# A hybrid decoder step on one core: quarter tiles for the sample attention, and its steps between k chunks of the second gate

## The chip, the cores and the metric

The kernel runs on one core of a Trainium2 chip. The metric is device time in microseconds (us), from the start to the end of one execution. TensorE (PE) multiplies, VectorE (DVE) and ScalarE (ACT) work elementwise, GpSimd (POOL) works elementwise and starts indirect DMAs, SyncE (SP) starts the weight loads. PE reads operands from SBUF and writes to eight PSUM banks: PS[0] and PS[1] of two banks each and PB of four.

## The reference, cut to what matters

One inference step of a decoder with two layers, of 512 + 16 prompt rows and 8 x 4 sample rows. Every sample row attends to the 256 best of 2048 cached keys and the new ones, which an index score picks; the cache is paged and is read through a page table. For the gates:

```python
z = x @ w_in
q, k, v, qi, ki, wi, h, bg, cg, ga, gb = jnp.split(z, offs, axis=-1)
u = cg * h                                   # convolved along the rows, times bg
logits = jnp.einsum('bqngd,bqjnd->bqngj', qg, kg).astype(jnp.float32) * (HEAD_DIM ** -0.5)
p = jax.nn.softmax(logits, axis=-1).astype(vg.dtype)
o = jnp.einsum('bqngj,bqjnd->bqngd', p, vg)
```

The attention's result times w_attn_out is multiplied with sigmoid(ga), the convolution's times w_conv_out with sigmoid(gb); the sum goes through w_o, a layer norm and a squared-ReLU MLP.

## The kernel before, in words

x (560 columns: 528 prompt rows and 32 sample rows) is kept transposed, split in a high and a low part (AXh, AXl). Every weight product is a *unit* (unit, L489 to L508): 128 output columns, 48 matmuls of 128x280, from 3 products of high and low parts, 8 k chunks and 2 halves of the rows. A weight slice of 512 KB is loaded by SP (load, L319), cast to its high part WH by ACT (high, L946) and subtracted to its rest WL by POOL (rest, L393), through two slots s = 0, 1. A unit of slot s writes PS[s], and the next one in that slot waits until it is evacuated (evac_done).

A layer runs through P1, keys and values, the queries of all heads, index scores, the prompt's top-k, GA (first gate), then the **head loop** (8 heads), the **conv stage** (w_conv_out, 8 units), the **sample attention**, AO (w_attn_out), WO and the MLP. Every engine has its own queue, in which the order is written out by hand; semaphores join them.

The head loop (PE L693 to L762, ACT L1153 to L1218, DVE L1580 to L1676): each head does the prompt attention of five row tiles (p_logits L713 and L714, p_transposes L726, p_values L738 on PE; p_exp, p_norm, p_out on ACT; p_max, p_inv, p_turned on DVE), with four units between: h, cg, bg and gb (the second gate) , all four of the same group of 128 columns. DVE multiplies h by cg (gate_c, L1627), convolves (short_conv, L1639 to L1643), multiplies by bg and splits (gate_b, L1648, L1404, L1405) into AHh and AHl. ACT turns gb into 1 + exp(-gb) in BB. DVE also does three of the 32 steps of the sample rows' top-k in each head (a pair of s_top L1572 and s_take L1575 on 32 x 2080 scores), four pairs before the loop and four in the conv stage. In the conv stage DVE does the reciprocals of BB (L1690) and multiplies the products by it (L1701).

The sample attention (PE L776 to L863) goes over g = 0, 1, four sequences each. POOL gathers (L439) the keys and then the values into KVB, two half tiles of 4 x 1 MB, which lie in AXh and AXl (h = 0) and in AHh and AHl (h = 1). PE transposes the keys into three banks (L797), ACT and DVE take turns at copying them to KTR (L1243, L1723), PE makes logits (L810, eight steps q), adds masks (L818) and the new keys (L826, L829); after DVE's maximum and ACT's exp come transposes of P (L838), values (L854) and transposes of the result (L861). DVE splits the result for AO (L1715, L1757, L1758); SG holds the first gate, whose reciprocals DVE does in this stage (L1690, L1725).

Of the kernel before, what the change touches and what calls it, by code (L numbers as in the profile page):

```python
# [22 lines left out]
P = 128  # L23
# [46 lines left out]
QH, GA, GATES, CONV, AO, WO, MLP = -1, 0, 1, 5, 6, 7, 8  # L70
# [14 lines left out]
def gate_use(k, c):  # L85


    return k % 2, c * 2 + (phase_use(k % 2, GATES) + k // 2)


def gate_slot_use(k, c):

    return c * 2 + (slot_use(GATES) + k // 2)
# [47 lines left out]
def trunk_program(nc, a):  # L141
    with ExitStack() as ctx:
# [10 lines left out]
        def at(name, shape, dt, off):  # L153
# [8 lines left out]
        KVB = [[at(f"KVB{h}{b4}", [P, TPP // 2, KV_W], F32, (off_axh, off_axl, off_ahh, off_ahl)[2 * h + b4 // 2]  # L162
                   + b4 % 2 * (TPP // 2 * KV_W * 4)) for b4 in range(4)] for h in range(2)]
# [82 lines left out]
        IDXH = sb("IDXH", [P, 2, NB], U32)  # L246
# [6 lines left out]
        HALF = [PS[i // 2][:, i % 2, 0:RH] for i in range(4)]  # L253
        V1 = PB[:, 2:4, 0:RH]
# [33 lines left out]
        kv_in = [[sem(f"kv_in{h}{b4}") for b4 in range(4)] for h in range(2)]  # L288
        kt_t, kt_ea, kt_ed, kt_mm = sem("kt_t"), sem("kt_ea"), sem("kt_ed"), sem("kt_mm")
# [18 lines left out]
        rows_k = a["cache_k"].rearrange("l n (s t) h d -> (l n s) (t h d)", t=TPP // 2)  # L308
        rows_v = a["cache_v"].rearrange("l n (s t) h d -> (l n s) (t h d)", t=TPP // 2)
# [8 lines left out]
        def _(sp):  # L318
# [32 lines left out]
            for l in range(DEPTH):  # L351
# [16 lines left out]
                with sp.Fori(0, KC) as c:  # L368
                    for k, col in enumerate((COL_H, COL_CG, COL_BG, COL_GB)):
                        s, n = gate_use(k, c)  # L370
                        load(s, l * USES[s] + n, wcol(w_in_v, l, c * P + col))
                for name, ph in (("w_conv_out", CONV), ("w_attn_out", AO), ("w_o", WO)):
# [19 lines left out]
        def _(pool):  # L392
# [12 lines left out]
            for l in range(DEPTH):  # L405
# [23 lines left out]
                with pool.Fori(0, 4 * (CONV + 1)) as i:  # L429
                    for s in range(2):  # L430
                        rest(s, l * USES[s] + i + phase_use(s, QH), s)
                for s in range(2):
                    rest(s, l * USES[s] + phase_use(s, CONV), s)

                def gather(g, h, rows):

                    for b4 in range(4):
                        b = 4 * g + b4
                        pool.indirect_dma_start(KVB[h][b4][:].rearrange("p t d -> p (t d)"), None, rows,  # L439
                                                bass.IndirectOffsetOnAxis(ap=IDXH[:, h, b:b + 1], axis=0)  # L440
                                                ).then_inc(kv_in[h][b4], 16)

                def products_done(ph):
                    for s in range(2):
                        pool.wait_ge(mm_done[s], l * SLOT_USES[s] + slot_use(ph) + 1)
                        apart(pool, started)

                products_done(CONV)
                gather(0, 0, rows_k)
                with pool.Fori(0, 3) as i:  # L450
                    for s in range(2):
                        rest(s, l * USES[s] + i + (phase_use(s, CONV) + 1), s)
                for s in range(2):
                    rest(s, l * USES[s] + phase_use(s, AO), s)
                products_done(AO)
                gather(0, 1, rows_k)
                for g in range(2):
                    if g == 1:
# [1469 lines left out]
```

## Time and profile before

| | us |
|---|---|
| time, three runs | 2591.24, 2593.61, 2595.88 (median 2593.61) |
| the profiled execution | 2593.55 |
| its span in the trace | 2591.8 |
| PE busy | 2324.9 (90%) |
| DVE busy | 1497.8 (58%) |
| ACT busy | 795.7 (31%) |
| POOL busy | 792.2 (31%) |

The profiled execution's own time is its span and 1.75 us around it. The page gives busy times of the engines, what the chain of work that ended last consists of, the costliest groups of instructions and the landing times of DMAs; the stages are told apart by windows of the trace, the order inside one by the timeline and the chain of waits. "PEclk" is the clock granted to TensorE, as a share of the full 2.4 GHz.

### The profile page before, as it was taken

The page shows a single profiled execution, that of the slowest core. Times are in us where ns is not written, and L with a number is a line of the kernel's source. Part 1 is how long each engine was busy: PE and PEld are TensorE (multiplying, and loading weights), DVE is VectorE, ACT ScalarE, POOL GpSimd, SP SyncE. Part 2 cuts the span into 40 slices and gives each one's busy share as a digit, 9 for nine tenths or more (in the row PEclk, how much of TensorE's full clock was granted, in tenths as well). Part 3 has the DMA queues.
Part 4 walks back from the last instruction along what each step waited for, and adds up shares of the span by engine and source line. Part 5 has one row for each costly group of instructions (what it writes and reads, how often), then busy time and mean ns, then how long its engine had stood idle before and what let it go on. Part 6 is the DMA issues. An engine that isn't in the chain of part 4 may idle for free.

```text
span 2591.8 us, 45648 instructions
## 1 busy us (share of the span) xinstructions
PE 2324.9 (90%) x17159; PEld 2134.2 (82%) x17159; DVE 1497.8 (58%) x2234; ACT 795.7 (31%) x1379; POOL 792.2 (31%) x384
## 2 busy tenths in 40 slices
PE   5988999998669899999899889999975899999995
PEld 4965988888339899999898489888953699999995
DVE  3759877778556632132586797777856566132145
ACT  2233333331111332222242443333221125122233
POOL 2410322234214323333443022222331252343440
PEclk9977999999779999999999699999997899999998
DMA  4420222225632322323333022222464232223230
GB/s 117 132 61 16 67 64 57 57 60 200 260 130 77 87 57 82 89 82 89 109 116 95 6 59 56 64 57 57 138 226 189 94 100 68 73 82 89 82 97 35
DMA packets 321366, 238.03 MB, mean 92 GB/s; under 512 B 9560, under 2 KB 309576, under 8 KB 313080
## 3 DMA queue, kind: packets, MB, share of 16 engines
q1 hardware_dynamic: 304424, 154.69, 21.5%
q0 software_dynamic: 12032, 77.07, 7.5%
q10 hardware_dynamic: 4816, 4.96, 0.6%
q8 instruction: 67, 1.10, 0.2%
q14 instruction: 27, 0.22, 0.0%
HBM read 231.73 MB, written 4.96 MB: 91 GB/s over the span
## 4 chain that ended last, share of the span: by engine, by line
PE 78%; DVE 11%; ACT 4%; issue 3%; DMA 2%; ACTq 1%; SPq 0%; DVEq 0%; POOL 0%; POOLq 0%
PE PS L504 54%; PE PS L489 9%; PE PS L797 3%; DVE BB L1690 2%; PE PB L714 2%; PE PS L623 2%; PE PB L738 2%; PE PB L810 1%; PE PS L854 1%; DVE SG L1690 1%; DVE SG L1725 1%; DVE SQ L1430 1%; DMA KVB<-in_cache_v_dram,IDXH 1%; DVE TKS L1575 1%; PE PB L726 1%
## 5 line engine op out<-in xcount | busy, mean ns | idle before, releaser
L395 POOL TENSOR_TENSOR WL<-ST,WH 128x1024 fp32r<-128x1024 f32 x290 | 705.2, 2433 | 1539.0 <-ACT WH L949 1539.0
L949 ACT CAST WH<-ST 128x1024 fp32r<-128x1024 f32 x290 | 303.7, 1047 | 1099.5 <-PE PS L504 944.1
L504 PE MATMUL PS<-AXh,WH 128*128 128x280 f32 x2688 | 575.6, 296 | 21.0 <-DVE AXl L1758 12.6
L504 PE MATMUL PS<-AXl,WH 128*128 128x280 f32 x2688 | 571.5, 294 | 0.0
L504 PE MATMUL PS<-AXh,WL 128*128 128x280 f32 x2688 | 566.5, 292 | 0.0
L504 PEld LDWEIGHTS PS<-AXh,WH 128*128 128x128 f32 x2688 | 432.0, 190 | 23.0 <-issue 21.6
L504 PEld LDWEIGHTS PS<-AXl,WH 128*128 128x128 f32 x2688 | 432.8, 191 | 0.0
L504 PEld LDWEIGHTS PS<-AXh,WL 128*128 128x128 f32 x2688 | 428.1, 190 | 0.0
L504 PE MATMUL PS<-AHh,WH 128*128 128x280 f32 x1152 | 242.0, 291 | 3.6 <-DVE AHl L1823 3.4
L504 PE MATMUL PS<-AHl,WH 128*128 128x280 f32 x1152 | 243.2, 292 | 0.0
L504 PE MATMUL PS<-AHh,WL 128*128 128x280 f32 x1152 | 241.0, 290 | 0.0
L1822 DVE TENSOR_TENSOR MT<-MT 128x560 f32<-128x560 f32 (+1 forms) x76 | 96.4, 1268 | 238.1 <-ACT AHh L1317 217.0
L504 PEld LDWEIGHTS PS<-AHh,WH 128*128 128x128 f32 x1152 | 182.9, 188 | 4.7 <-DVE AHl L1823 3.8
L504 PEld LDWEIGHTS PS<-AHl,WH 128*128 128x128 f32 x1152 | 183.7, 189 | 0.0
L504 PEld LDWEIGHTS PS<-AHh,WL 128*128 128x128 f32 x1152 | 181.7, 188 | 0.0
L797 PEld LDWEIGHTS PS<-ident,KVB 128*128 128x128 f32 x512 | 69.5, 166 | 103.3 <-DVE KTR L1723 42.8
L1782 DVE TENSOR_TENSOR X<-X,PS 128x560 f32 (+2 forms) x60 | 37.2, 620 | 201.8 <-PE PS L504 165.2
L797 PE MATMUL PS<-ident,KVB 128*128 128x128 f32 x512 | 84.8, 323 | 75.5 <-DVE KTR L1723 39.8
L1572 DVE MAX8 top<-TKS 32x8 f32<-32x2080 f32 x64 | 147.3, 2302 | 3.2 <-DVE TKS L1575 2.9
L1575 DVE MATCH_REPLACE8 TKS<-top,TKS 32x2080 f32<-32x2080 f32 x64 | 147.0, 2297 | 0.0
L489 PE MATMUL PS<-AXh,WH 128*128 128x280 f32 x384 | 119.1, 310 | 19.3 <-DVE AXl L1447 10.0
L489 PE MATMUL PS<-AHh,WH 128*128 128x280 f32 x384 | 116.3, 303 | 3.8 <-issue 3.8
(249 smaller groups left out, 3476.9 us busy)
## 6 DMA issues: line engine op xcount, KB each, us to landing
ST<-in_w_in_dram SPq DMA_DIRECT2D x114, 512.0 KB, 3.8
ST<-in_w_up_dram SPq DMA_DIRECT2D x64, 512.0 KB, 4.0
ST<-in_w_down_dram SPq DMA_DIRECT2D x64, 512.0 KB, 3.8
ST<-in_w_conv_out_dram SPq DMA_DIRECT2D x16, 512.0 KB, 3.8
ST<-in_w_attn_out_dram SPq DMA_DIRECT2D x16, 512.0 KB, 3.7
ST<-in_w_o_dram SPq DMA_DIRECT2D x16, 512.0 KB, 3.8
NAT<-in_x_prompt_dram SPq DMA_DIRECT2D x4, 512.0 KB, 3.7
o_y_dram<-NAT ACTq DMA_DIRECT2D x4, 512.0 KB, 2.6
```

The lines of the kernel that those rows point to most:

```text
L395: pool.tensor_tensor(WL[slot][:, :, :], ST[s][:, :, :], WH[slot][:, :, :].bitcast(F32), ALU.subtract).then_inc(lo_done[s], 1)
L489: mm = pe.matmul(out, x[:, k, :], y[:, k, r0:r1], start=(k == 0 and y is hi and x is WH[slot]), stop=(k == KC - 1 and y is lo))
L504: mm = pe.matmul(out[:, h, 0:RH], x[:, k, :], y[:, k, RH * h:RH * h + RH], start=(k == 0 and y is hi and x is WH[slot]), stop=(k == KC - 1 ...
L623: mm = pe.matmul(PS[j % 2][0:n, k0 // 512, 0:k1 - k0], x[hp, c0:c0 + n], y[hp, k0:k1], start=(i == 0), stop=(i == 2))
L714: mm = pe.matmul(bank, QST[:, c0:c0 + m], KT[:, n, k0:k1], start=False, stop=True)
L738: mm = pe.matmul(PB[:, 3, 0:m], VN[0:k1, kt, HD * n:HD * n + HD], PPT[i % 2][0:k1, m * kt:m * kt + m], start=(kt == 0), stop=(kt == keys(r ...
L797: tr = pe.transpose(banks[t % 3][:, P * j:P * j + P], KVB[c // 2][b4][:, 4 * (c % 2) + j, HD * n:HD * n + HD], ident[:, :])
L949: act.copy(WH[slot][:, :, :], ST[s][:, :, :]).then_inc(hi_done[s], 1)
L1572: own.link(dve.max(top[0:RS, 0, :], TKS[:, :]), alone=True)
L1575: own.link(dve.match_replace(TKS[:, :], top[0:RS, 0, :], TKS[:, :], NEG_TAKEN), alone=True)
L1690: own.link(dve.reciprocal(v, v))
L1822: own.link(dve.tensor_tensor(h, h, h, ALU.mult))
```

## The change

The second gate's products (gb) leave the head loop, whose heads come in pairs now, with three units each cut at k chunks (6 matmuls of 128x280 each) and in another order on all engines. DVE's top-k pairs are moved: none before the loop, two in even heads and three in odd ones, twelve in the conv stage. ACT copies conv's products to BB. The 64 k chunks of the gb units are laid between the steps of the sample attention, all through PS[0]; ACT's exp goes to a buffer GE, DVE does its reciprocal and multiplies BB by it. Keys and values are gathered in quarter tiles (16 of 4 x 0.5 MB a layer instead of 8 halves of 4 x 1 MB) through two buffers in AHh and AHl, since AXh and AXl are wanted by the gb products; POOL's gathers wait for the last reader of a buffer, and the rests of the gb weights stand between them. All copies to KTR are on ACT. The first AO unit waits for the split of the sample columns in its second half alone. Cut to its core (SP's loads follow the new order of units):

```diff
-        KVB = [[at(f"KVB{h}{b4}", [P, TPP // 2, KV_W], F32, (off_axh, off_axl, off_ahh, off_ahl)[2 * h + b4 // 2]
-                   + b4 % 2 * (TPP // 2 * KV_W * 4)) for b4 in range(4)] for h in range(2)]
+        KVB = [[at(f"KVB{s}{b4}", [P, 4, KV_W], F32, o + 4096 * b4) for b4 in range(4)]
+               for s, o in enumerate((off_ahh, off_ahl + 1536))]
+        assert off_ahl == off_ahh + BIG
+        GE = at("GE", [P, R], F32, off_ahh + 16384)
...
+            return (PS[1][:, 0, :], PS[1][:, 1, :], PB[:, 2, :])[t % 3] if t < 16 else PS[1][:, 1 - t % 2, :]
...
+                def gather(j):
+                    g, c, rows = j // 8, j % 4, (rows_k, rows_v)[j // 4 % 2]
+                    for b4 in range(4):
+                        pool.indirect_dma_start(KVB[j % 2][b4][:].rearrange("p t d -> p (t d)"), None, rows,
+                                                bass.IndirectOffsetOnAxis(ap=IDXH[:, c, 4 * g + b4:4 * g + b4 + 1], axis=0)
+                                                ).then_inc(kv_in[j % 2][b4], 16)
...
-                products_done(CONV)
-                gather(0, 0, rows_k)
-                with pool.Fori(0, 3) as i:
-                    for s in range(2):
-                        rest(s, l * USES[s] + i + (phase_use(s, CONV) + 1), s)
-                for s in range(2):
-                    rest(s, l * USES[s] + phase_use(s, AO), s)
-                products_done(AO)
-                gather(0, 1, rows_k)
-                for g in range(2):
-                    if g == 1:
-                        for h in range(2):
-                            pool.wait_ge(pv_mm, l * 10 + 2 * h + 2)
-                            apart(pool, started)
-                            gather(1, h, rows_k)
-                    for h in range(2):
-                        pool.wait_ge(kt_t, l * 64 + 32 * g + 16 * h + 16)
-                        apart(pool, started)
-                        gather(g, h, rows_v)
+                    pool.wait_ge(mm_done[s], l * SLOT_USES[s] + slot_use(GB) + 1)
+                    apart(pool, started)
+                gather(0)
+                gb_rest(1)
+                gather(1)
+                gb_rest(2)
+                for c in range(4):
+                    k_read(0, c)
+                    gather(2 + c)
+                gb_rest(3)
+                v_read(0, 0)
+                gather(6)
+                v_read(0, 1)
+                gather(7)
+                gb_rest(4)
+                v_read(0, 2)
+                gather(8)
+                gb_rest(5)
+                v_read(0, 3)
+                gather(9)
+                gb_rest(6)
+                for c in range(3):
+                    k_read(1, c)
+                    gather(10 + c)
+                gb_rest(7)
+                k_read(1, 3)
+                gather(13)
+                v_read(1, 0)
+                gather(14)
+                rest(0, l * USES[0] + phase_use(0, AO), 0)
+                v_read(1, 1)
+                gather(15)
+                rest(1, l * USES[1] + phase_use(1, AO), 1)
...
                         p_logits(0)
-                        gate(0)
+                        gate(0, 0, 5)
                         p_transposes(0)
                         p_logits(1)
                         p_logits(2)
-                        gate(1)
+                        gate(0, 5, 8)
+                        gate(1, 0, 2)
                         p_transposes(1)
                         p_logits(3)
                         p_values(0)
+                        gate(1, 2, 6)
                         p_transposes(2)
                         p_values(1)
-                        gate(2)
+                        gate(1, 6, 8)
+                        gate(2, 0, 2)
                         p_logits(4)
                         p_transposes(3)
                         p_values(2)
-                        gate(3)
+                        gate(2, 2, 8)
                         p_transposes(4)
                         p_values(3)
                         p_values(4)
...
+                def gb_products(n):
+                    for _ in range(n):
+                        u, k = gb_k[0] // KC, gb_k[0] % KC
+                        s = u % 2
+                        if k == 0:
+                            pe.wait_ge(lo_done[s], l * USES[s] + phase_use(s, GB) + u // 2 + 2)
+                            if u == 0:
+                                pe.wait_ge(evac_done[0], l * PAIR_USES + slot_use(GB) + 1)
+                            else:
+                                pe.wait_ge(evac_done[1 - s], l * PAIR_USES + slot_use(GB) + (u - 1) // 2 + 2)
+                        mm = pair_products(PS[0], s, AXh, AXl, k)
+                        if k == KC - 1:
+                            mm.then_inc(mm_done[s], 1)
...
+                    for q in range(8):
+                        for t in range(4 * q + 2, min(4 * q + 6, 32)):
+                            k_transposes(t)
+                            if g == 1 and q % 2 == 1 and t == 4 * q + 3:
+                                gb_products(1)
+                        gb_products(1)
+                        logits(q)
+                        if g == 1 and q == 1:
+                            o_transposes(0)
+                    if g == 0:
+                        pe.wait_ge(masks_ready, l + 1)
+                        apart(pe, started)
+                        for c in range(4):
+                            mask(c)
...
+                    gb_products((6, 4)[g])
+                    pt_transposes(0)
+                    pt_transposes(1)
+                    gb_products((2, 4)[g])
+                    values(0)
+                    gb_products(4)
+                    pt_transposes(2)
+                    values(1)
+                    if g == 0:
+                        gb_products(6)
+                    pt_transposes(3)
+                    values(2)
+                    if g == 0:
+                        gb_products(6)
+                    pt_transposes(4)
+                    values(3)
+                    values(4)
...
+                    p_exp(3)
+                    p_out(0)
+                    p_norm(3)
+                    p_out(1)
                     high_only(1)
-                    p_out(0)
-                    p_exp(3)
-                    p_out(1)
-                    p_norm(3)
+                    p_exp(4)
+                    p_out(2)
+                    act.copy(QST[:, :], Q[:, bass.ds((c + 1) % KC if hh else c + 1, 1), 0:RP].rearrange("p o r -> p (o r)")).then_inc(qst_done, 1)
+                    p_norm(4)
                     high_only(2)
-                    p_exp(4)
-                    p_norm(4)
-                    act.copy(QST[:, :], Q[:, bass.ds((c + 1) % KC, 1), 0:RP].rearrange("p o r -> p (o r)")).then_inc(qst_done, 1)
-                    p_out(2)
-                    minus_exp(*gate_n(3), BB, c)
                     p_out(3)
-                    plus_one(1, l * PAIR_USES + gate_slot_use(3, c), BB, c)
                     p_out(4)
...
+                        evac(s, l * USES[s] + i + phase_use(s, CONV), l * SLOT_USES[s] + i + slot_use(CONV),
+                             lambda: act.copy(halves(BB[:, bass.ds(i * 2 + s, 1), :].rearrange("p o r -> p (o r)")),
+                                              PS[s][:, :, 0:RH]))
...
+                def gb(u):
+                    s = u % 2
+                    high(s, use(s, phase_use(s, GB) + u // 2 + 1), s, l * SLOT_USES[s] + slot_use(GB) + u // 2 + 1)
+                    act.wait_ge(mm_done[s], l * SLOT_USES[s] + slot_use(GB) + u // 2 + 2)
+                    if l * KC + u > 0:
+                        act.wait_ge(gb_mul, l * KC + u)
+                    apart(act, started)
+                    act.activation(halves(GE[:, :]), PS[0][:, :, 0:RH], ACT.Exp, scale=-1.0).then_inc(evac_done[s], 1)
+                    act.wait_ge(evac_done[s], l * PAIR_USES + slot_use(GB) + u // 2 + 2)
+                    act.activation(GE[:, :], GE[:, :], ACT.Identity, bias=one[:, 0:1]).then_inc(inv_done, 1)
...
+                    if g == 0:
+                        k_copies(0, 32)
+                        gb(1)
+                    else:
+                        k_copies(0, 10)
+                        o_columns(0)
+                        k_copies(10, 22)
+                        gb(5)
+                        k_copies(22, 32)
...
+                    pt_copy(0)
+                    pt_copy(1)
+                    gb((2, 6)[g])
+                    pt_copy(2)
+                    if g == 0:
+                        gb(3)
+                    pt_copy(3)
+                    if g == 0:
+                        gb(4)
+                    pt_copy(4)
+                    if g == 1:
+                        gb(7)
...
-                with own.fori(4, 2) as i:
-                    s_top()
-                    s_take()
...
-                    s_top()
-                    s_take()
+                    if hh == 1:
+                        s_top()
+                        s_take()
                     p_turned(1)
                     p_max(3)
                     p_turned(2)
+                    p_inv(3)
                     gate_c()
-                    p_inv(3)
+                    apart(dve, started)
                     s_top()
-                    short_conv()
-                    apart(dve, started)
-                    s_take()
                     p_max(4)
                     p_turned(3)
                     p_inv(4)
+                    s_take()
+                    short_conv()
+                    apart(dve, started)
                     gate_b()
                     p_turned(4)
...
-                with own.fori(4, 4) as i:
+                with own.fori(12, 2) as i:
                     s_top()
                     s_take()
-                    for s in range(2):
-                        sigmoid(chunk(BB, i * 2 + s))
-                        dve.wait_ge(mm_done[s], l * SLOT_USES[s] + i + (slot_use(CONV) + 2))
-                        bb = halves(chunk(BB, i * 2 + s))
-                        dve.tensor_tensor(bb, PS[s][:, :, 0:RH], bb, ALU.mult).then_inc(evac_done[s], 1)
...
+                def gb(u):
+                    dve.wait_ge(inv_done, l * 16 + KC + u + 1)
+                    sigmoid(GE[:, :])
...
+                    if g == 0:
+                        gb(1)
+                        gate_a(0)
+                        gate_a(1)
+                        gb(2)
+                        gate_a(2)
+                        gb(3)
+                    else:
+                        gate_a(7)
```

Here gate(k, k0, k1) issues the products of chunks k0 to k1 - 1 of one unit, gb_products(n) the next n chunks of the gb units, gb_rest(u) the rest of the weights of gb unit u on POOL, and gate_a(c) is DVE's reciprocal of one chunk of the first gate.

## Rows read from the trace of the kernel before

**Rows 1.** Windows by stage: us, busy us by engine, PEclk, DMA share, GB/s.

```profile
366.30:402.10 35.80, 34.82 (x256) 31.94 (x255) 25.66 (x45) 13.55 (x31) 9.51 (x5) 1.00 0.23 59
581.00:636.50 55.50, 50.03 (x386) 49.54 (x386) 53.27 (x30) 8.80 (x10) 24.27 (x14) 0.99 0.45 155
636.50:776.30 139.80, 92.11 (x737) 54.20 (x737) 75.21 (x91) 24.14 (x56) 26.31 (x27) 0.79 0.55 214
1896.40:2039.60 143.20, 94.59 (x737) 55.34 (x737) 75.36 (x91) 24.13 (x56) 26.40 (x27) 0.77 0.53 209
1351.00:1359.00 8.00, 8.00 (x64) 8.00 (x64) 7.79 (x12) 1.91 (x3) 6.95 (x6) 1.00 1.03 410
```

**Rows 2.** Timeline of PE: starts of two heads, of conv and of AO.

```profile
365.77 0.38 PE L713 MATMUL PB<-MP,identb 16*16 16x512 bf16 x1
...
401.52 0.38 PE L713 MATMUL PB<-MP,identb 16*16 16x512 bf16 x1
...
581.48 0.50 PE L504 MATMUL PS<-AHh,WH 128*128 128x280 f32 x2
...
776.27 0.81 PE L504 MATMUL PS<-AXh,WH 128*128 128x280 f32 x2 [6.28 <-DVE AXl L1758]
```

**Rows 3.** Chain of waits of the third head: units on PE (start, us, what).

```profile
367.35 6.37 PE PS L504 x48
...
384.25 6.21 PE PS L504 x48
...
392.32 6.19 PE PS L504 x48
```

**Rows 4.** Timeline of DVE in the second half of that head.

```profile
384.05 0.86 DVE L1627 TENSOR_TENSOR UE<-PS,UE 128x280 f32<-128x280 f32 x3
...
385.67 2.30 DVE L1572 MAX8 top<-TKS 32x8 f32<-32x2080 f32 x1
...
393.78 0.69 DVE L1596 TENSOR_REDUCE stp<-PB 128x1 f32<-128x512 f32 x1 [0.23 <-DVE TKS L1575]
...
395.60 0.74 DVE L1648 TENSOR_TENSOR CY<-PS,CY 128x560 f32<-128x560 f32 x1
...
397.06 0.74 DVE L1405 TENSOR_TENSOR AHl<-CY,AHh 128x560 f32 x1
398.97 0.69 DVE L1616 COPY PPT<-PB 128x512 f32<-128x512 f32 x1 [1.17 <-PE PB L726]
```

**Rows 5.** Timeline of ACT in the first half of that head.

```profile
371.00 0.74 ACT L1188 ACTIVATE PP<-PP,stp 16x528 f32<-16x528 f32 x1 [1.75 <-DVE stp L1605]
...
376.23 0.84 ACT L1188 ACTIVATE PP<-PP,stp 128x128 f32<-128x128 f32 x2
```

**Rows 6.** Windows of PE around idle stretches: us, busy, PEclk, DMA share, GB/s.

```profile
289.60:292.80 3.20, 0.00 (x0) 1.00 0.18 53
292.80:298.60 5.80, 5.78 (x28) 0.71 0.34 90
631.20:636.70 5.50, 0.00 (x0) 0.87 0.20 60
636.70:642.10 5.40, 5.33 (x25) 0.50 1.05 403
...
735.70:737.40 1.70, 1.64 (x12) 1.00 1.03 429
```

**Rows 7.** DMA issues of the page: KB each, median us to landing.

```profile
IKB<-in_cache_idx_k_dram,IDX POOLq DMA_INDIRECT x16, 6.2
```

**Rows 8.** Timeline of POOL: one of the issues of a gather.

```profile
582.29 0.94 POOL L439 DMA_INDIRECT KVB<-in_cache_k_dram,IDXH  x1 [0.30 <-issue]
```

**Rows 9.** Timeline of PE: key transposes of two periods, values of a quarter.

```profile
644.35 2.10 PE L797 MATMUL PS<-ident,KVB 128*128 128x128 f32 x16 [0.76 <-ACT KTR L1243]
...
648.21 2.10 PE L797 MATMUL PS<-ident,KVB 128*128 128x128 f32 x16 [0.44 <-ACT KTR L1243]
...
678.27 1.93 PE L854 MATMUL PS<-KVB,KTR 128*32 128x256 f32 x32
```

More of the change, by code:

```diff
@@ L431, in _ @@
                         rest(s, l * USES[s] + i + phase_use(s, QH), s)
-                for s in range(2):
[L433 to L441, printed above, removed]
@@ new lines, in gb_rest @@
+                def gb_rest(u):
+                    rest(u % 2, l * USES[u % 2] + phase_use(u % 2, GB) + u // 2, u % 2)
+                def gather(j):
[4 more added lines that the diff above has]
+                                                ).then_inc(kv_in[j % 2][b4], 16)
@@ new lines, in k_transposes @@
+                        if g == 1 and t < 2:
+                            pe.wait_ge(pt_e, l * 10 + 4 + t)
+                        bank = k_bank(t)
+                        if t >= 3:
+                            pe.wait_ge(kt_e, l * 64 + 32 * g + (t - 2 if t < 16 else 14 if t == 16 else 16 if t == 17 else t - 1))
+                        for j in range(4):
+                            tr = pe.transpose(bank[:, P * j:P * j + P], KVB[c % 2][b4][:, j, HD * n:HD * n + HD], ident[:, :])
+                        tr.then_inc(kt_t, 1)
@@ new lines, in mask, with logits @@
+                    def mask(c):
+                        pe.matmul(PB[:, c, :], selb[:, g, :], MS[:, 512 * c:512 * c + 512], start=False,
+                                  stop=True).then_inc(ls_mm, 1)
+                    def logits(q):
+                        c, n = q // KVH, q % KVH
+                        pe.wait_ge(kt_e, l * 64 + 32 * g + 4 * q + 4)
+                        if g == 1 and q == 6:
+                            pe.wait_ge(ot_e, l * 2 + 1)
+                        apart(pe, started)
@@ new lines, in _ @@
+                    if g == 0:
+                        pe.wait_ge(masks_ready, l + 1)
+                        apart(pe, started)
+                        for c in range(4):
+                            mask(c)
+                    for b4 in range(4):
+                        for m in range(KVH):
+                            pe.matmul(new_l[32 * b4:32 * b4 + 32, :],
+                                      QP[:, 4 * g + b4, m].rearrange("p h s -> p (h s)"),
+                                      KT[:, m, RP:R], start=(m == 0), stop=False)
@@ new lines, in gate_a @@
+                def gate_a(c):
+                    dve.wait_ge(inv_done, l * 16 + KC)
+                    sigmoid(SG[:, c, :])
+                def gb(u):
+                    dve.wait_ge(inv_done, l * 16 + KC + u + 1)
+                    sigmoid(GE[:, :])
+                    dve.tensor_tensor(BB[:, u, :], BB[:, u, :], GE[:, :], ALU.mult).then_inc(gb_mul, 1)
+                gb(0)
+                for g in range(2):
+                    for c in range(4):
+                        dve.wait_ge(ls_mm, l * 10 + 5 * g + c + 1)
+                        dve.reduce_max(st[:, c:c + 1], PB[:, c, :], AX_X)
+                        if g == 1 and c < 2:
+                            gate_a(5 + c)
+                        if g == 1 and c == 2:
+                            gb(5)
```

301 lines of the change are left out of this document (153 added, 148 removed).

## The prediction

> **What bounds the kernel now.** I read the page first: PE is busy 90% of the span, DVE 58%, so what counts is where PE waits. Then I cut the trace into the stages that the change touches. In a head [rows 1] PE is busy 34.82 of 35.80 us at full clock, DVE 25.66. In the conv stage DVE fills 53.27 of 55.50, and PE's 50.03 end early. In the sample attention PE is busy 92.11 of 139.80 at a mean clock of .79: the gaps and the lowered clock are there. From the first conv product to the first of AO it is 194.8 us in layer 0 (581.48 to 776.27 [rows 2]) and some 198.2 in layer 1, whose attention stage is 143.2 for 139.8 [rows 1].
>
> Then the chain of waits of one head [rows 3]: four weight units on PE, 6.2 us each, and attention steps between them; the head lasts 35.75 (401.52 less 365.77 [rows 2]). VectorE's timeline [rows 4] shows that this is a near thing: from gate_c at 384.05 DVE works with hardly a gap until gate_b's last split ends at 397.80, and PE's fourth unit ends at 392.32 + 6.19 = 398.51. So a head has two chains: PE's four units, and "second unit (cg) done, then 14 us of DVE, then the last values". The fourth unit hides the second chain with .7 us to spare.
>
> **The head loop.** Taken out: unit gb, 6.2 us of PE in each of 16 heads, 99 us, which come back in the attention stage. What a head lasts then is read from the DVE chain. Let T be its first product, G the end of the second unit. Before G stand the same PE steps as now ahead of the third unit: 384.25 less 365.77, 18.5 us. But they are cut in k chunks (6.19 over 8, .77 each) and come in another order. p_transposes(0) now stands after 5 chunks, at T + 1.6 + 4.0 = T + 5.6, while p_norm(0) ends at 371.74, T + 6.0 [rows 5]: stall .4. p_transposes(1) needs p_norm(1), which stands on ACT behind the cast that waits for the end of gate 0 (367.35 + 6.37 = 373.72): its row starts at 376.23 and the first of its two ends near 376.65, 2.9 after gate 0. Now a whole unit lies between, then two chunks (1.55): stall 1.4. So G = T + 20.3.
>
> After G the changed DVE order is, from start to start in [rows 4]: gate_c with the column copies 1.6, s_top, short_conv and s_take together 8.1, p_max(4) to p_inv(4) 1.8, gate_b with its splits 2.2, p_turned(4) .7: 14.4. PE's own work after G (8 chunks and the last attention steps) is about 9.4, so PE ends 5 us early and waits. Then p_values(4) 1.1 and .1 to start. An even head lasts 20.3 + 14.4 + 1.2 = 35.9. In an odd head a third top-k pair stands ahead of p_turned(1) and p_max(3); p_exp(3) waits for that, p_out(0) stands behind p_exp(3) on ACT, and p_values(1) needs the bank that p_out(0) frees: about 1.0 more. Mean 36.4, against 35.75: .65 to .7 a head, **+11** in all. With no stall before G it would be 34.1 (-1.6 a head); with both stalls and the pair's 5 us fully uncovered half the time, 38.4 (+2.7): I take the sum, since the pair has PE's second unit beside it.
>
> So gb leaves, and its 6.2 us become waiting and some more. That has a second price. After 3.2 us without work ahead of the first head the granted clock of the next 5.8 us is .71 (1.00 would have done that work in 4.1: 1.7 lost); after 5.5 idle at the end of conv PE ran 5.4 us of work at .50, the lower of the two levels (1.2 GHz), 2.7 lost [rows 6]. A head with 5 us of waiting lies between these; the .4 stall comes from DVE and ACT and so hides part of the loss. From 1.0 to 2.3 a head, I take 1.3, near the first row: **+21**. After the 2.8 idle up to 735.70 the clock stayed at 1.00 [rows 6], so nothing is the other end.
>
> The four pairs ahead of the loop go (some 21 us of DVE), but PE runs other products beside them, and 3.2 us before the first head is all that PE idles there [rows 6]: between nothing and 3 us a layer, and the first unit hides DVE's start, so nothing.
>
> **The conv stage.** ACT takes the products by a copy, DVE's reciprocals and multiplies leave the stage, and the 5.5 us that PE waits at its end [rows 6] go. PE is then the bound: 8 x 6.19 = 49.5, and the first GB unit follows, to s + 55.7 (s is the start of conv). DVE's 12 pairs at 5.3 are 64 us, to s + 66, beside conv and the keys; the masks are wanted only after all logits of g = 0. Price nothing.
>
> **The gathers.** Both K and both V tiles used to have buffers of their own, in pieces of 1 MB; g = 0's first keys were fetched beside conv. Now the two buffers lie in AH, which conv reads, so the first fetch starts at s + 49.5. POOL needs 4 x 1.24 = 5.0 for a tile [rows 8], and the nearest landing is that of IKB's pieces, of the same size and row length: median 6.2 [rows 7]. First piece near s + 57, PE idle 1 to 3. Afterwards each fetch waits for the last reader of its buffer: 11.2 from release to the last landing, against the 8 to 10 us that PE works on the other buffer. POOL's gb_rest (about 2.4 each) stand between the issues and hold them back.
>
> **Keys, g = 0.** A period of q is 3.86 now (648.21 less 644.35), in which transposes are 2.10 and PE waits .4 to .8 for copies [rows 9]. A chunk adds .77, of which that wait swallows half: 4.25 with three banks (first half), 5.05 with two banks and all copies on ACT. 8 q: 37 us; with the first tile s + 95.
>
> **Rest of g = 0.** 24 chunks 18.6; transposes of P, masks and new keys 4; values 4 x 1.93 and .6 [rows 9]; and a wait for the next GB unit, whose rest stands on POOL behind a gather that waits for values: 4.6. Sum 36, s + 131. **Keys, g = 1:** 37, four more chunks 3.1, and ACT's gb(5) between copies 3: s + 174. **Rest of g = 1:** 12 chunks 9.3, transposes and values 11, the last unit waiting for the bank that ACT's exp frees 3.2, the last two V tiles fetched late 4 to 10 (6 taken), and 3 from the last values to AO, since the prompt columns are split earlier (6.28 idle stand there now [rows 2]). Sum 33, s + 207. Against 194.8 and 198.2: 12 and 9, **+21**. That the stage takes 99 us of products for 21 is the gain of the change; it loses that in the head.
>
> The Trainium skill, "DMA: Bandwidth & Descriptors", section "Measured (HBM→SBUF, 128 partitions, SWDGE, issued from GpSimd)", says that a DMA should carry 1 MiB or more for 75% of the peak, which speaks against the halved pieces. Here it does not show: with eight pieces of .5 MB in flight a window moved 410 GB/s [rows 1].
>
> **Sum.** 2593.55 (the profiled execution; span 2591.8 and 1.75 around it; .06 under the median of the runs shown) + 11 + 21 + 21 = **2647**.
>
> **Rivals.** (a) **The other side**: DVE's chain isn't last in a head. If G comes without stalls and the DVE tail runs beside PE's third unit, PE bounds the head and 6.2 us leave each: 99 less; with 21 for the attention 2516, and 2560 if half of it comes. For it: PE is 97% busy in the head. Against: the tail has no gaps in [rows 4], 13.75 from gate_c to gate_b's end. It decides from the point where the tail after G is shorter than PE's 9.4. (b) **The clock holds** in the heads: 2626. For it: the 2.8 idle at 733 that cost nothing. Against: both longer idles of [rows 6]. (c) **The attention comes near PE's own bound**: conv 49.5, GB 49.5, 92.11 at .79 (73 at full clock), 5 to 8 of waits: s + 177 to 180, some 16 a layer less than now: 2593.55 + 32 - 33 = 2593. For it: the chunks fill just those waits that lowered the clock. Against: one bank for GB, two buffers for all tiles, one queue for rests and gathers. (d) **The halved pieces run at half the rate**: 10.2 us instead of 5.1 for the 2 MB of a tile (at 410 GB/s), on some six exposed tiles a layer 30: 2707. The rule of the skill named above would give this; the 410 GB/s speak against it.
>
> **How the numbers follow.** My forecast .60, (a) .08, (b) .15, (c) .12, (d) .05. The forecast's own bounds: a head -1.6 to +2.7 without the clock, the clock 0 to 2.3, the attention -10 to +25 a layer. These don't fall together; the range takes in (b) and the upper half of the way from (c) to the forecast, and reaches up as far: 2600 to 2690. A measurement tells about .2% (5 us) from no change. Faster: (a) and a part of (c), .13; same: the middle of (c), .04; slower: .83.
>
> **What would show it.** In the profile after: PE idle of about 5 us ahead of the last p_values of each head, ended by DVE's p_turned; a granted clock below 1.00 in a head's window; a head of 36 to 38 in place of 35.75; no reciprocal in conv, and PE at once in GB products after it; AO's first product near s + 207; a .5 MB piece landing after some 6 us. The prediction is wrong where heads last under 34, or where AO starts before s + 190.

## The result, and the profile after

The changed kernel takes 2764.57 us (median of four runs, 2760.74 to 2768.59), beside 2592.43 for the kernel before: a ratio of 1.066, with a 95% interval from 1.064 to 1.069. The forecast was 2647 in a range of 2600 to 2690, so the sign was right, and the slowdown is 172 us instead of 54. The profiled execution took 2768.07 with a span of 2766.3, 174.5 more than the span before.

From the page of the changed kernel: busy times by engine, and the granted clock in 40 slices of the span.

```profile
PE 2391.5 (86%) x17143; PEld 2179.0 (79%) x17159; DVE 1511.1 (55%) x2154; ACT 839.9 (30%) x1479; POOL 850.8 (31%) x448
...
PEclk8969888778999999999998698888799899999998
```

The granted clock of the kernel before, in its own 40 slices:

```profile
PEclk9977999999779999999999699999997899999998
```

The same work on PE takes longer, and the low digits of the clock (7 and 8) stand in two stretches that were at 9 before, the head loops (slices 5 to 10 and 25 to 29 of the changed kernel). Windows by stage of the changed kernel show it: the heads of layer 0, layer 0 from conv to AO, the heads of layer 1, and one head alone (columns as in [rows 1]).

```profile
290.40:646.50 356.10, 268.62 (x1650) 235.24 (x1658) 219.49 (x352) 87.23 (x216) 56.68 (x25) 0.81 0.14 37
646.50:866.00 219.50, 190.37 (x1507) 150.13 (x1507) 137.20 (x96) 76.49 (x139) 99.94 (x80) 0.94 0.60 192
1638.70:1992.00 353.30, 265.78 (x1652) 232.87 (x1661) 220.29 (x354) 87.56 (x218) 56.59 (x25) 0.82 0.14 37
...
377.25:423.63 46.38, 35.59 (x207) 31.36 (x208) 24.90 (x42) 10.99 (x27) 7.05 (x3) 0.76 0.13 34
```

The same stages of the kernel before:

```profile
292.80:581.50 288.70, 280.20 (x2043) 257.06 (x2043) 207.56 (x364) 108.49 (x241) 76.82 (x34) 0.99 0.22 58
581.50:776.30 194.80, 141.73 (x1121) 103.60 (x1121) 127.98 (x118) 32.86 (x66) 50.11 (x40) 0.85 0.52 198
```

So the account of the 174.5 is: head loops 67.5 and 64.1 us longer (131.6, or 8.2 for each of the 16 heads: 44.3 on the mean against 36.1, from the first head's first product to conv's, over eight); conv to AO 24.3 and 24.4 longer (219.1 and 222.6); the rest 5.8 shorter, as the first heads start earlier (by 2.4 in layer 0, by 3.5 after the stage before in layer 1). The four pairs that no longer stand ahead of the loops may be the reason; these runs don't show it, because in the runs below, none of which has these pairs ahead of the loop, the same two stretches differ among each other by 2.4 and 7. The forecast had 32 for the head loops and 21 for conv to AO. It is the heads that were missed most.

In the third head of layer 0, one of the longer ones (46.4 us), [rows 2 to 4] turn into the following. DVE, POOL and PE in the timeline of the changed kernel (start, us):

```profile
404.22 2.38 DVE L1787 COPY CSO<-UE 128x2 f32 x1
...
413.87 2.22 DVE L1796 TENSOR_SCALAR CY<-UE,PL 128x528 f32<-128x528 f32 x1 [0.26 <-DVE TKS L1735]
...
420.74 0.68 DVE L1773 COPY PPT<-PB 128x512 f32<-128x512 f32 x1
```

```profile
404.21 2.36 POOL L415 TENSOR_TENSOR WL<-ST,WH 128x1024 fp32r<-128x1024 f32 x1 [11.31 <-ACT WH L1062]
413.46 2.34 POOL L415 TENSOR_TENSOR WL<-ST,WH 128x1024 fp32r<-128x1024 f32 x1 [6.89 <-ACT WH L1062]
```

```profile
412.59 0.63 PE L780 MATMUL PB<-ident,PP 128*128 128x128 f32 x4 [1.53 <-ACT PP L1303]
...
421.66 2.04 PE L792 MATMUL PB<-PPT,VN 128*128 128x128 f32 x8 [7.77 <-DVE PPT L1773]
```

PE waits 7.8 us ahead of the last values for DVE's p_turned(4): the chain that the prediction named. But two instructions of it are far longer than in its sum. A copy of two columns takes 2.38 us, until POOL's subtraction (the rest of a weight slice) that began .01 earlier is over, and the tensor_scalar of the short convolution takes 2.22, again until .3 behind the end of POOL's next one. In each of the 16 heads one of gate_c's three column copies waits like this (2.1 to 2.4 us). Beside these stand the windows of PE alone (us, busy, PEclk, DMA share, GB/s): the head's first logits, its second unit, the end of gate 2, the wait, and the last values.

```profile
377.30:379.90 2.60, 2.60 (x8) 0.50 0.00 0
...
395.00:400.80 5.80, 5.80 (x25) 0.50 0.23 69
...
403.00:412.50 9.50, 7.99 (x57) 1.00 0.21 55
414.00:421.60 7.60, 0.00 (x0) 0.53 0.26 69
421.66:423.60 1.94, 1.94 (x8) 0.50 0.00 0
```

After the wait the last values and the next head's logits run at the lower level (1.2 GHz), as [rows 6] had it. What [rows 6] did not have: the clock falls a second time in the same head, for most of the second unit (395.0 to 400.8), after a wait of 1.4 us at 390.9. This second fall is not in every head: nine of the 16 have it, between 15 and 24 us after the head's start, and last 43.6 to 47.6 us; the seven others last 41.8 to 43.2. The head behind the one shown is one of the seven:

```profile
423.63:466.86 43.23, 31.87 (x207) 27.45 (x207) 29.36 (x45) 10.88 (x27) 7.05 (x3) 0.86 0.14 36
```

### The profile page after: what moved, and what is told of

Read it like the earlier page. It is cut to its first block, busy times and chain, and to the rows that moved or that the text cites. A ratio compares the mean times of both kernels' runs of the same rounds, so it can differ in the third digit from the quotient of the medians.

```text
span 2766.3 us, 45468 instructions
## 1 busy us (share of the span) xinstructions
PE 2391.5 (86%) x17143; PEld 2179.0 (79%) x17159; DVE 1511.1 (55%) x2154; ACT 839.9 (30%) x1479; POOL 850.8 (31%) x448
## 4 chain that ended last, share of the span: by engine, by line
PE 71%; DVE 11%; issue 7%; ACT 6%; DMA 2%; POOL 2%; ACTq 1%; DVEq 0%; SPq 0%; POOLq 0%
PE PS L551 48%; PE PS L532 9%; PE PB L792 2%; PE PB L768 2%; PE PS L669 2%; DVE top L1732 2%; PE PS L876 2%; POOL KVB L463 1%; DVE TKS L1735 1%; PE PB L890 1%; DMA KVB<-in_cache_k_dram,IDXH 1%; PE PB L942 1%; ACT KTR L1371 1%; DVE UE L1790 1%; DVE SQ L1590 1%
## 5 line engine op out<-in xcount | busy, mean ns | idle before, releaser
L551 PE MATMUL PS<-AXh,WH 128*128 128x280 f32 x2656 | 593.1, 306 | 22.2 <-POOL WL L415 9.3
L551 PE MATMUL PS<-AXh,WL 128*128 128x280 f32 x2656 | 574.9, 299 | 0.0
L551 PEld LDWEIGHTS PS<-AXh,WH 128*128 128x128 f32 x2656 | 439.7, 197 | 28.6 <-issue 16.8
L551 PEld LDWEIGHTS PS<-AXl,WH 128*128 128x128 f32 x2656 | 440.2, 196 | 0.0
L551 PEld LDWEIGHTS PS<-AXh,WL 128*128 128x128 f32 x2656 | 438.9, 196 | 0.0
L551 PE MATMUL PS<-AHh,WH 128*128 128x280 f32 x1152 | 243.5, 293 | 3.4 <-DVE AHl L1979 3.4
L792 PE MATMUL PB<-PPT,VN 128*128 128x128 f32 (+2 forms) x480 | 86.3, 320 | 125.3 <-DVE PPT L1773 123.9
L792 PEld LDWEIGHTS PB<-PPT,VN 128*128 128x128 f32 (+1 forms) x480 | 78.7, 236 | 133.1 <-issue 128.3
L532 PE MATMUL PS<-AXh,WH 128*128 128x280 f32 x416 | 130.3, 313 | 17.3 <-DVE AXl L1607 9.9
L532 PE MATMUL PS<-AXh,WL 128*128 128x280 f32 x416 | 126.0, 303 | 0.0
```

The source lines that it names most:

```text
L532: mm = pe.matmul(out, x[:, k, :], y[:, k, r0:r1], start=(k == 0 and y is hi and x is WH[slot]), stop=(k == KC - 1 and y is lo))
L551: mm = pe.matmul(out[:, h, 0:RH], x[:, k, :], y[:, k, RH * h:RH * h + RH], start=(k == 0 and y is hi and x is WH[slot]), stop=(k == KC - 1 ...
L792: mm = pe.matmul(PB[:, 3, 0:m], VN[0:k1, kt, HD * n:HD * n + HD], PPT[i % 2][0:k1, m * kt:m * kt + m], start=(kt == 0), stop=(kt == keys(r ...
```

## The experiments

**POOL and DVE apart.** In DVE's order of a head:

```diff
-  gate_c()          # with its three column copies
-  s_top()
+  gate_c()          # without them
+  s_top()
+  columns()
   p_max(4); p_turned(3); p_inv(4)
-  s_take()
   short_conv()
+  s_take()
   gate_b()
```

> The changed kernel with two moves in DVE's order of a head: gate_c's three column copies stand after s_top, and short_conv stands ahead of s_take. All instructions stay. Theory A (DVE's copies and its tensor_scalar sit out POOL's 2.4 us subtraction when they meet it): the first copies and the tensor_scalar of 128x528 go back from 2.4 and 2.22 us to .17 and .50, 3.8 us a head leave the DVE chain, 16 x 3.8 = 61, so about 2700. Theory B (they are long for another reason, such as the lowered clock or the loop's unrolling): the durations stay and the time stays at 2765.

Measured: 2685.33, 79 less, ratio to the kernel before 1.035 (1.029 to 1.041). The same tensor_scalar, in all 16 heads (min/median/max ns), after and here:

```profile
L1796 DVE TENSOR_SCALAR CY<-UE,PL x16: 2215/2224/2230, 322.6 to 1980.4; 128x528 f32<-128x528 f32 x16
```

```profile
L1799 DVE TENSOR_SCALAR CY<-UE,PL x16: 495/496/499, 318.2 to 1906.8; 128x528 f32<-128x528 f32 x16
```

Theory A holds. Heads are 39.6 on the mean, 4.7 less: 3.8 of it is the two waits, the rest came with a clock of .88 for .81 in the heads' window. In this kernel s_top (2.30) runs beside POOL's subtraction and is no longer for it.

**A filler for PE.** Ahead of the last values of a head:

```diff
   p_values(3)
+  # into the bank of the unit cg, once gate_c has read it
+  for j in range(48):
+      pe.matmul(PS[s1][:, j % 2, 0:RH], AXh[:, j // 6, 0:P], AXl[:, j // 6, 0:RH], start=True, stop=True)
   p_values(4)
```

> The changed kernel with 48 products of 128x280 more in each head, which nobody reads (AXh by AXl into the bank of the unit cg, after gate_c has read it), ahead of the last p_values, where PE waits 7.8 us for DVE. Theory A (the lowered clock costs time on the chain ahead of G and in the last values): 6.2 us more work for PE makes the heads shorter, by 3 to 6 us each, since the granted clock of a head's window goes from .81 towards 1.00: 2670 to 2715. Theory B (the clock's loss is hidden behind DVE's chain): 2765, or slower where the filler overruns its gap.

Measured: 2706.95, 58 less, ratio 1.043 (1.039 to 1.048). With 6.2 us more work a head lasts 41.3, 3.0 less. The window of its eight heads, at .97 for .81:

```profile
290.00:620.50 330.50, 289.00 (x2042) 261.15 (x2043) 218.46 (x352) 86.99 (x217) 57.01 (x25) 0.97 0.15 40
```

Theory A: the lowered clock is a loss of its own on the chain, some 3 us a head. Between the two profiled runs lie 64 us, 48 of them in the heads; another 11 are from conv to AO (214.1 and 216.3), a stage that the edit leaves as it is.

**Both.** The first edit and a filler of 36 products.

> The kernel of e1_port (DVE's copies and tensor_scalar away from POOL's subtraction) with 36 products of 128x280 more ahead of the last p_values, which nobody reads, to fill PE's wait there. Theory A (port and clock are two separate losses, and what is left is the sum of the prediction): heads go from 39.3 to between 36.4 (the prediction's sum without the clock's price) and 37.2 (e2_filler's 41.0 less the 3.8 of the port), total 2638 to 2655. Theory B (the clock's price vanished with the port's waits): heads stay at 39 or get longer by what the filler overruns.

Measured: 2645.79, heads 37.0 on the mean, at this clock in those of layer 0:

```profile
291.30:588.90 297.60, 276.49 (x1947) 251.66 (x1947) 187.03 (x352) 88.12 (x217) 57.13 (x25) 0.97 0.17 45
```

Theory A: the two losses nearly add up (4.7 and 3.0 alone, 7.3 together), and with most of both gone a head lasts .9 longer than before; the prediction's sum without the clock's price was .7. In some heads of this run the clock does not fall at all: even ones last 35.8 to 35.9 and odd ones 36.7, where the prediction, without the clock, had 35.9 and 36.9. One of each:

```profile
440.39:476.31 35.92, 33.34 (x244) 30.34 (x243) 20.86 (x42) 10.99 (x27) 7.11 (x3) 1.00 0.16 45
476.31:513.00 36.69, 33.59 (x245) 30.38 (x244) 25.44 (x45) 11.00 (x27) 7.10 (x3) 1.00 0.17 44
```

**A short tail for DVE.** In a head of the changed kernel (gate_c again without its copies):

```diff
   p_turned(1)
   p_max(3)
+  s_top(); s_take()
   p_turned(2); p_inv(3)
   gate_c()
-  s_top()
   p_max(4); p_turned(3); p_inv(4)
-  s_take()
+  columns()
   short_conv(); gate_b(); p_turned(4)
   # and no third pair in odd heads: 16 pairs in the conv stage
```

> The changed kernel with another DVE order in a head: the pair s_top, s_take that stood after gate_c stands after p_max(3), in the 6.9 us that DVE waits there, the third pair of odd heads goes to the conv stage (16 pairs there), and the column copies stand after p_inv(4). Theory A (a head lasts G plus DVE's tail): the tail shrinks from 18.4 to about 9.5, as long as PE's own work there, PE hardly waits and the clock stays up: heads of 31 to 34 in place of 44, 2765 - 16 x 11 = 2590, at best 2560. Theory B (the lost time is the price of cutting units in chunks and the order on PE, or G moves back by the pair's 5 us): heads of 39 or more, over 2680.

Measured: 2667.05 in the profiled run (a second run took 2707.73; the heads are those of the first), heads of 35.8 at first, 41.0 and 42.1 at the end of layer 0, 38.0 on the mean. That is neither: shorter by 6, but not by 11. The trace shows why. DVE's second split, which takes .74 in [rows 4], meets POOL's third subtraction in all 16 heads, and PE waits for what stands behind it. The longer heads come with a lower clock: .94 in the first, .79 in the seventh of layer 0.

```profile
431.58 2.67 DVE L1565 TENSOR_TENSOR AHl<-CY,AHh 128x560 f32 x1
```

```profile
431.29 2.36 POOL L415 TENSOR_TENSOR WL<-ST,WH 128x1024 fp32r<-128x1024 f32 x1 [5.22 <-ACT WH L1062]
```

```profile
435.12 1.77 PE L792 MATMUL PB<-PPT,VN 128*128 128x128 f32 x8 [3.94 <-DVE PPT L1773]
```

**The tail mended.** On top of that:

```diff
-  gate_b(); p_turned(4)
+  p_turned(4); gate_b()            # DVE
-  evac(gate 0); p_exp(1); p_exp(2); p_norm(1); p_norm(2)
+  p_exp(1); p_exp(2); p_norm(1); p_norm(2); evac(gate 0)   # ACT
```

> The kernel of e3_tail with two more moves in a head: DVE turns P of the last tile (p_turned(4)) ahead of gate_b, so that the last values no longer wait for gate_b's splits, of which the second one stood 2.67 us for .74 beside POOL; and ACT does p_exp and p_norm of tiles 1 and 2 ahead of the evacuation of the unit h. Theory A (a head is the longer of PE's work and the chain to the last values; stalls lower the clock): PE waits 4 us less at the end and 1.4 less ahead of p_transposes(1), heads of 31 to 33, full clock, near 2575. Theory B (PE's own order and the cut units hold a head at 36): 2640 or more.

Measured: 2541.02 (2539.8 to 2542.49), ratio .980 (.978 to .981): faster than the kernel before, and than theory A's 2575. The split takes .74 again in all heads. Between the first and the last head of a layer, heads are 29.65 in place of 35.75, so nearly all of the 6.2 us of the unit gb leaves each of them. A window of 30.9 us, from the third head into the fourth:

```profile
363.40:394.30 30.90, 29.63 (x216) 26.83 (x215) 22.86 (x46) 11.05 (x28) 8.30 (x4) 1.00 0.19 51
```

Theory A: PE is busy 96% at full clock. PE's instructions and their order are those of the changed kernel, so cutting the units costs nothing that can be seen here. From conv to AO it takes 219.7 and 218.0, near the 219.1 and 222.6 of the changed kernel; this stage is what is left of the loss.

**Fewer chunks in the attention.** In the changed kernel, chunks 1 to 6 of each unit of the second gate are left out:

```diff
+  if k in (0, KC - 1):
       mm = pair_products(PS[0], s, AXh, AXl, k)
```

> The changed kernel without 6 of the 8 k chunks of each unit of the second gate (chunks 0 and 7 stay), so 48 chunks of .77 us fewer a layer in the attention; the loads, casts, rests, gathers and all orders stay. Theory A (PE's work sets the pace of the attention, 219 us from conv to AO): some 37 us less a layer, 182, and the total near 2690. Theory B (the turnover of the two gather buffers sets it: 11 us from release to landing of each of 16 tiles, POOL's queue): 205 or more, total above 2735. The trace shows which waits take the place of the chunks.

Measured: 2744.95 in a single run, and 209.9 and 209.6 us from conv to AO, 9.2 and 12.9 less for 37 us less work. That speaks for theory B's number. The longest waits of PE in that stage are the following: first those of the changed kernel, then those without the chunks (us in total, times, longest).

```profile
PE PS L876 <- ACT KTR L1371: 11.0, 19, 3.1
PE PB L942 <- DMA KVB<-in_cache_v_dram,IDXH: 5.5, 6, 1.7
PE PS L551 <- POOL WL L415: 4.6, 1, 4.6
PE PS L876 <- DMA KVB<-in_cache_k_dram,IDXH: 3.1, 4, 1.1
```

```profile
PE PS L877 <- ACT KTR L1372: 11.0, 19, 3.1
PE PS L877 <- DMA KVB<-in_cache_k_dram,IDXH: 9.5, 7, 3.9
PE PS L551 <- POOL WL L415: 8.7, 1, 8.7
PE PB L943 <- DMA KVB<-in_cache_v_dram,IDXH: 7.3, 8, 1.9
```

The waits for gathers and for POOL's rest grow by 12 us where the chunks were, and the clock falls from .94 to .86 over the stage, so that PE's busy time is 163.7 us, 27 less than before for 37 us less work at full clock:

```profile
647.40:857.20 209.80, 163.66 (x1217) 116.81 (x1217) 134.62 (x96) 76.78 (x138) 99.92 (x80) 0.86 0.63 201
```

Theory B's mechanism stays open by this: the waits show that gathers hold PE where it has less to do, not that they set the pace with the chunks in place, where PE is busy 190 of 219 us.

**Earlier gathers.** On top of the mended heads:

```diff
   for b4 in range(4):
+      read(b4)          # K: wait for kt_t of this sequence alone; V: for a count after this sequence
       pool.indirect_dma_start(KVB[j % 2][b4] ...)
   # values: loops over b4 outside, j inside; gb_rest(1), (4), (5) one place earlier or later in POOL's queue
```

> The kernel of e5_heads with gathers that wait for a quarter of their buffer instead of all of it (K: each piece for the transposes of its own sequence; V: the values loop runs over sequences outside, so that a piece is free early), and with POOL's rests of units 1, 4 and 5 moved one place in its queue. Theory A (the turnover of the two buffers sets the pace of the attention): pieces are issued up to 3 us earlier for some 12 tiles a layer, 15 to 25 us less a layer from conv to AO than e5_heads (which should stand near 219). Theory B (PE's work or the copies set it): within 5 us of e5_heads a layer.

Measured: 2545.01, and 223 us from conv to AO in both layers, so theory B by the number. But the edit had a cost of its own. With the sequence loop outside, 32 products of the values take 4.59 us where they took 1.93, both at a clock of 1.00; here and in the kernel with the mended heads:

```profile
639.90 4.59 PE L942 MATMUL PB<-KVB,KTR 128*32 128x256 f32 x32
```

```profile
638.80 1.93 PE L942 MATMUL PB<-KVB,KTR 128*32 128x256 f32 x32
```

So this run alone doesn't decide. **The loops put back** (V's gathers wait for whole tiles again):

> The kernel of e6_turn with the loops of the values back in the old order (sequences inside), so that V's gathers wait for the whole tile again; K's pieces still wait for a quarter each, and POOL's rests stand as in e6_turn. In e6_turn 32 products of the values took 4.59 us for 1.93, 21 us a layer, and the stage was only 4 us longer than in e5_heads. Theory A (the earlier issues and the moved rests did gain some 16 us a layer there, which the slower values ate): 200 to 208 us from conv to AO instead of 219, total 2510 to 2525. Theory B (the values of e6_turn only filled time in which PE would have waited for gathers anyway): 215 or more, total within 8 us of 2541.

Measured: 2531.79, ratio .978 (.975 to .980), 214.5 and 216.4 from conv to AO: 5.3 and 1.6 less than with the mended heads alone. The total is 9.2 less, just outside B's 8 and short of A's range. Nearer to B: the earlier issues and the moved rests are worth a few microseconds a layer, not sixteen.

**More buffers for the copied keys.** On top of the mended heads, for g = 1:

```diff
-  act.copy(KTR[t % 4][:, :], k_bank(t))        # from t = 4 on behind the logits that read it
+  act.copy(KTB[g][t % (4 + 4 * g)][:, :], k_bank(t))
```

> The kernel of e5_heads with eight buffers instead of four for the copied keys of the second group (g = 1; the four more lie in the tile of the probabilities, which is free then). Theory A (with all copies on ACT, the four copies of step q + 1 wait for the logits of step q, since there are just four buffers: .6 x 4 and two semaphore waits a step, so that a step lasts 5.3 to 5.7 and not PE's 4): the keys of g = 1, 45 to 46.5 us now, last 36 to 41, and 10 to 16 us leave the total. Theory B (the landing of the gathers sets that phase): 43 or more, the total within 6 us of 2541; e6_turn, which started them earlier, then should have gained.

Measured: 2528.24, ratio .975 (.973 to .977). The keys of g = 1 fall from 46.6 and 45.0 to 42.9 and 42.2, and the waits for the copies in them from 6.2 to 3.6 us, of which 3.1 is ACT's own gb(5): the wait existed, but behind it stands PE's work (36.9 us busy of 42.9). From conv to AO 3.1 and 2.3 us are gained, 5.4 of the 12.8 by which the total fell. Between the two profiled runs, 10.9 apart, another 3.9 lie in a stretch that the edit leaves as it is, from AO of layer 1 to the end: 553.4 and 549.4, and 548 to 552 in the other runs here. So that the total fell by theory A's 10 to 16 is in part luck. The phase itself stays above theory A's 41.

**All of it.**

> The kernel of e9_order with the eight buffers of e7_ktr for the keys of g = 1. Theory A (both waits are real and separate): 3 to 6 us a layer less than e9_order. Theory B (what one of them frees the other takes): within 2 us a layer of e9_order.

Measured: 2522.13 (2515.12 to 2527.78), ratio .974 (.971 to .977), 211.8 and 214.4 from conv to AO, 2.7 and 2.0 less than without the eight buffers. It lies under theory A's 3 and at B's edge, and untouched stretches differ by more between runs: not decided. This version is 70 us faster than the kernel before.

## Why the prediction was right or wrong

**Right: what bounds the head.** That the DVE chain behind the second unit would set a head's length, and PE wait at its end, is in the trace: the wait ends with p_turned, 7.8 us long where 5 was said. With POOL's waits and most of the clock's loss taken out (e8_both), a head lasts .9 longer than before; the sum without the clock had .7, and even and odd heads come out as it said.

**Wrong: the tail's 14.4 us.** The step that failed is "from start to start in [rows 4]". It took the durations of the copies (.17) and of the tensor_scalar (.49) from places where POOL had no subtraction running, and kept them for another order. The changed order puts gate_c right behind the second unit, whose end also releases, over ACT's cast, POOL's subtraction; and short_conv behind s_take, where the end of the third unit releases the next subtraction in the same way. Measured: 3.8 us a head by the rows, 4.7 a head by e1_port, with the clock that comes with it; 79 us in all. The prediction asked what POOL's rests hold back in POOL's queue, not what they hold back on DVE. The Trainium skill has the rule: "SBUF — State Buffer", section "SBUF: two separate sides", says that VectorE and GpSimd share a pair of ports as an exclusive lock, which a VectorE instruction needs in its two-port mode, or with two SBUF inputs against a GpSimd instruction that reads SBUF, and that the loser waits for all of the other's instruction. The rows agree: an SBUF-to-SBUF copy, a tensor_scalar and a tensor_tensor of two SBUF tiles waited (2.38 for .17, 2.22 for .50, 2.67 for .74), s_top beside POOL did not.

**Wrong in size: the clock.** 1.3 us a head were put in, near the first of [rows 6], with 2.3 as the upper end. Measured: 3.0 (after against e2_filler) and 2.6 (e1_port against e8_both), both from below, since the clock is at .97 and not at 1.00 in the runs with a filler. The term saw one fall of the clock a head; in nine heads of 16 there are two, and the last values run at the lower level too, on the chain (2.04 us for 1.13). Rival (b), that the clock holds, fell with it.

**Wrong in size: the attention.** 207 was said, 219.1 and 222.6 measured. By its parts in layer 0, from conv's first product: keys of g = 0 start at 57 (57 to 59 said) and end at 99 (95); the rest of g = 0 takes 37 (36), the keys of g = 1 45.5 (43), the rest 37 (33). No step of it is far off. In g = 0 the periods from one q to the next are 4.2 to 5.1 (the last 3.7), as said; what the sum lacks there is the start, 8.2 us from the first transposes to the first logits, with three waits for pieces of the first tile (1.07, .79 and .63). The largest term, 4 us in layer 0 and 6 in layer 1, is the rest of g = 1: the clock is .86 there (.83 in layer 1), and most of the products of the last two tiles of values run at the lower level (3.53 and 3.62 us for 26 of 32, where all 32 take 1.93 at full clock), for which the sum had nothing. Rival (c), the stage near PE's bound, fell. Rival (d), pieces at half the rate, fell too: the page of the changed kernel has them landing after 6.3 and 6.2 us, as [rows 7] had it for IKB's. The 410 GB/s that spoke against it come from a window in which at most five of its eight pieces were in flight at a time, and not eight; and the rule of the Trainium skill that the prediction quotes names no rate for half a MiB, so that half the rate was the prediction's own reading of it. The second of the two stretches of values, and the landings:

```profile
859.95 3.62 PE L942 MATMUL PB<-KVB,KTR 128*32 128x256 f32 x26 [0.17 <-DMA KVB<-in_cache_v_dram,IDXH]
```

```profile
KVB<-in_cache_k_dram,IDXH POOLq DMA_INDIRECT x64, 6.3
KVB<-in_cache_v_dram,IDXH POOLq DMA_INDIRECT x64, 6.2
```

**Rival (a)**, the gain of 99 us in the heads, had the right mechanism and the right point from which it decides: once the tail behind G is as short as PE's own work there (e5_heads), 6.1 us leave a head, 95 in all with the first and last ones, and the total is 2541, where the rival said 2516 with the attention at its forecast (by the same sum half of the 99 gives 2565, not the 2560 written there). It did not happen in the change as it stands.

Put together, the profiled execution after took 121 us more than the forecast: in the heads 96 for port and clock (7.3 a head measured for both, less the 1.3 said for the clock, by 16) and 3 for the .9 in place of .7; in the attention 28; by the earlier first heads 6 less, a term that the prediction put at nothing.

## What to carry to other kernels

A duration taken from a trace is that of its neighbours too: before an instruction is moved, look which instruction of the engine that shares its port to SBUF runs beside it now, and which would then. Taking work from the engine that is the bound gains only as far as the other chain of the stage is shorter, or is shortened in the same edit; here five moves in DVE's and ACT's order made 224 us of difference with PE's program untouched. Where a wait opens on TensorE, count the lowered clock after it on the chain, and not only for the longest wait: here it fell a second time in nine heads of 16.

## What the runs showed of the hardware

A small instruction waits as long as a large one: a copy of 128x2 took 2.38 us beside POOL's subtraction, a tensor_scalar of 128x528 2.22. More work made the heads shorter: 6.2 us a head of products that nobody reads took 3.0 us off each head, at a granted clock of .97 in place of .81. And the order of two loops over the same 32 small products (128x32 weights, each sequence into its own 32 rows of the output) made 4.59 us of 1.93, when successive products went to the same rows instead of taking turns. One such product takes .38 us in both orders (median), so the 1.93 are products that run beside each other.
